# Attention stage of a one-core encoder: the decode tile moved inside each head, the two maps of differential attention scored one after the other, and the first head's loads cut in halves

## The reference, cut to what matters

```python
# A, stick-breaking
w = exp(log_sigmoid(z) + after)          # after: reversed cumulative sum of -softplus(z)
# B, sliding window of 128 with sinks; the two query chunks of a tile see 2 blocks of keys at most
p = softmax(concat[s + bias, sink])[:-1]
# C, differential: two maps of 32 dimensions for each head, one shared V
w = softmax(s[0] + bias) - lam * softmax(s[1] + bias);  out = rmsnorm(w @ v, gain)
# D, forgetting
p = softmax(s + f_q - f_k)
```

## Time and profile before

| | us |
|---|---|
| median of 3 runs (1962.41 to 1962.87) | 1962.59 |
| the profiled execution | 1961.66 |
| its span from first to last instruction | 1959.9 |
| PE busy in the span | 1828.4 |
| DVE busy | 850.5 |
| ACT busy | 650.0 |
| the stretch from 350 to 900 us, which holds the attention stage: PE busy | 475.32 of 550 |

### The profile page before, as it was taken

How to read it: one execution, slowest core, us unless ns; L and a number is a source line. 1 busy time by engine, 2 the same in 40 slices (tenths; PEclk the granted TensorE clock), 3 DMA queues, 4 the chain that set the end, 5 groups by cost and what they waited for, 6 DMA issues and landing times. The chain is left out here.

```text
span 1959.9 us, 27322 instructions
## 1 busy us (share of the span) xinstructions
PE 1828.4 (93%) x10459; PEld 1637.6 (84%) x10459; DVE 850.5 (43%) x1619; ACT 650.0 (33%) x1387; POOL 85.1 (4%) x169
## 2 busy tenths in 40 slices
PE   6999998588889999979989999999999999998998
PEld 6999996477777787868889898989898989996886
DVE  4333331666665666543543333333333333333434
ACT  5322321566554444442332121212121222221335
POOL 0000000000000010011010000000000000000000
PEclk9999999699899999979989999999999999999999
DMA  5666841756456745625231111111111111112102
GB/s 178 210 226 218 269 170 67 154 122 138 97 121 146 146 103 132 148 60 184 70 126 44 43 44 44 43 44 43 43 43 44 43 43 43 43 44 66 50 28 99
DMA packets 152165, 195.20 MB, mean 100 GB/s; under 512 B 42980, under 2 KB 106148, under 8 KB 152024
## 3 DMA queue, kind: packets, MB, share of 16 engines
q1 hardware_dynamic: 105352, 131.63, 25.8%
q10 hardware_dynamic: 39136, 36.05, 5.5%
q0 software_dynamic: 7552, 25.76, 4.0%
HBM read 143.17 MB, written 54.81 MB: 101 GB/s over the span
## 5 line engine op out<-in xcount | busy, mean ns | idle before, releaser
L113 PE MATMUL up<-xt_hi,w_hi_even 128*128 128x384 f32 x768 | 258.0, 336 | 2.0 <-PEq L1444 1.8
L115 PE MATMUL up<-xt_hi,w_lo_even 128*128 128x384 f32 x768 | 257.8, 336 | 0.0
L114 PE MATMUL up<-xt_lo,w_hi_even 128*128 128x384 f32 x768 | 257.6, 335 | 0.0
L115 PE MATMUL down<-w_hi_odd_b,hidden_lo 128*128 128x512 f32 x576 | 224.5, 390 | 0.0
L114 PE MATMUL down<-w_lo_odd_b,hidden_hi 128*128 128x512 f32 x576 | 224.5, 390 | 0.0
L113 PE MATMUL down<-w_hi_odd_b,hidden_hi 128*128 128x512 f32 x576 | 224.0, 389 | 0.0
L1665 DVE TENSOR_TENSOR h_rows<-down,h_rows 128x1024 f32<-128x1024 f32 x72 | 88.2, 1225 | 236.8 <-PE down L115 236.8
L1630 ACT ACTIVATE hidden_rows<-up 128x384 f32<-128x384 f32 x96 | 47.3, 492 | 418.0 <-PE up L115 418.0
L1658 DVE TENSOR_TENSOR hidden_rows<-hidden_rows 128x384 f32<-128x384 f32 x96 | 53.6, 558 | 224.3 <-ACT hidden_rows L1630 224.3
L113 PEld LDWEIGHTS up<-xt_hi,w_hi_even 128*128 128x128 f32 x768 | 145.0, 189 | 3.6 <-DVE xt_lo L140 2.2
L114 PEld LDWEIGHTS up<-xt_lo,w_hi_even 128*128 128x128 f32 x768 | 145.0, 189 | 0.8
(11 more groups left out here) (264 smaller groups left out, 3522.0 us busy)
## 6 DMA issues: line engine op xcount, KB each, us to landing
w_raw<-w_up SPq DMA_DIRECT2D x64, 256.0 KB, 2.9
w_raw<-w_down SPq DMA_DIRECT2D x64, 256.0 KB, 3.2
w_raw<-w_in SPq DMA_DIRECT2D x24, 256.0 KB, 4.5
head_rows<-head_out ACTq DMA_DIRECT2D x16, 288.0 KB, 3.8
head_rows_in<-head_rows POOLq DMA_DIRECT2D x9, 512.0 KB, 4.4
x_rows<-x_prompt SPq DMA_DIRECT2D x8, 512.0 KB, 3.6
w_raw<-w_out SPq DMA_DIRECT2D x16, 256.0 KB, 5.5
residual_rows<-x_prompt POOLq DMA_DIRECT2D x16, 256.0 KB, 3.2
```

Of the source, the lines that this page charges most:

```text
L113: nc.tensor.matmul(out, xh, wh, start=first, stop=False)
L114: nc.tensor.matmul(out, xh, wl, start=False, stop=False)
L115: return nc.tensor.matmul(out, xl, wh, start=False, stop=last)
```

## The change

- Order: the first head keeps its order; in the other 15 the sample's tile comes after the tile of 640 keys and before that of 768 (the sixth of nine). `tile(i)` takes the place of `i % TILES`; all that hung on the sample's tile as the last of its head (C's norm, the stores) now hangs on `ends_head`. POOL squares C's outputs before it spreads the next head's new weights, and norms after that. In A, DVE copies the sample's output between the first and the second large operation of the tile three steps later.
- C's maps: for more than 512 keys PE waits for map 0's buffer, issues map 0's matmuls and adds, signals, and then does the same for map 1. Up to 512 keys, and for the sample, the two maps still alternate.
- Fillers: 3 for every tile of C (was 7 for the four wide ones).
- Semaphores: no initial increments and no `primed_sem`; waits for nothing are left out.
- First head: keys and queries come in two halves, 6 transfers of columns 0 to 511, then 6 of columns 512 to 1151. PE starts after the first 6 (`first_in`) and waits for the others ahead of its fifth tile.

```diff
+            FIRST_ORDER = list(range(TILES))
+            LATER_ORDER = [0, 1, 2, 3, 4, SAMPLE, 5, 6, 7]
+            def order(job):
+                return LATER_ORDER if job else FIRST_ORDER
+            def tile(i):
+                return order(i // TILES)[i % TILES]
...
             def is_sample(i):
-                return i % TILES == SAMPLE
+                return tile(i) == SAMPLE
+            def ends_head(i):
+                return i % TILES == TILES - 1
...
-            def at(name, k):
-                return (TILES if name == "o_full" else 1) + k
+            def after(eng, name, k):
+                if k > 0:
+                    eng.wait_ge(q[name], k)
...
                 def _(sp):
-                    sp.wait_ge(primed_sem, 1)
...
+                                if job == 0:
+                                    for cols, loaded in ((slice(0, 512), first_in), (slice(512, TILES * P), done)):
+                                        for part, to in ((0, at_hi), (1, at_lo)):
+                                            sp.dma_start(kt[to:to + half, x, cols].bitcast(F32), k2[g][part][of_k, cols]).then_inc(loaded, 16)
+                                            sp.dma_start(qt[0][to:to + half, x, cols].bitcast(F32), q2[g][part][of_q, cols]).then_inc(loaded, 16)
+                                        for part, to in ((1, at_hi), (0, at_lo)):
+                                            sp.dma_start(qt[1][to:to + half, x, cols].bitcast(F32), q2[g][part][of_q, cols]).then_inc(loaded, 16)
+                                    continue
...
-                    for name in NAMES:
-                        pool.sem_inc(q[name], TILES if name == "o_full" else 1)
-                    pool.sem_inc(primed_sem, 1)
...
                         for job in range(len(JOBS)):
+                            of_c = job and JOBS[job - 1][0] == "C"
+                            if of_c:
+                                squares(job - 1)
                             spread_new(job)
+                            if of_c:
+                                norm(job - 1)
                             if job + 1 < len(JOBS):
                                 spread_operands(job + 1)
-                            if JOBS[job][0] == "C":
-                                norm(job)
...
                         nc.vector.scalar_tensor_tensor(b, z, 0.0, b, ALU.max, ALU.add).then_inc(q["a_sp"], 1)
+                        if between is not None:
+                            out(between)
...
+                        if i == 0:
+                            pe.wait_ge(first_in, 16 * 6)
+                        if (i == 4 if job == 0 else t == 0):
+                            job_loaded(pe, job)
...
+                        if g == "C" and n > 512:
+                            for m in maps:
+                                bank_free(m)
+                                products([m])
+                                add(m)
+                            return
+                        for m in maps:
+                            bank_free(m)
...
-                        wide = 4 <= t < SAMPLE
...
-                        for _ in range({"A": 3 if t >= 3 else 1, "B": 2, "C": 7 if wide else 3, "D": 0}[g]):
+                        for _ in range({"A": 3 if t >= 3 else 1, "B": 2, "C": 3, "D": 0}[g]):
```

More of the change, by code:

```diff
@@ L784, in keys @@
             def keys(i):
-                n = P * (i % TILES + 1)
+                n = P * (tile(i) + 1)
                 if is_sample(i):
@@ L1171, in maximum @@
                                 src = probs(i)
-                                nc.vector.scalar_tensor_tensor(src[:, 0:n], score(i, m)[:, 0:n], fq[:, odd(i), i % TILES:i % TILES + 1], cs[odd(i)][:, 0:n],
+                                nc.vector.scalar_tensor_tensor(src[:, 0:n], score(i, m)[:, 0:n], fq[:, odd(i), tile(i):tile(i) + 1], cs[odd(i)][:, 0:n],
                                                                ALU.add, ALU.subtract).then_inc(q["f_scores"], 1)
-                                dve.wait_ge(q["f_scores"], at("f_scores", sum(gated(y) for y in range(i + 1))))
+                                after(dve, "f_scores", sum(gated(y) for y in range(i + 1)))
                             if g != "B":
@@ L1312, in scores @@
-                            pe.wait_ge(q[f"ks_in{e}"], at(f"ks_in{e}", 16 * sum(cache_loads(JOBS[x][0]) for x in range(e, job + 1, 2))))
+                            after(pe, "spread", 3 * (job + 1))
+                            after(pe, f"ks_in{e}", 16 * sum(cache_loads(JOBS[x][0]) for x in range(e, job + 1, 2)))
                         maps = range(2 if g == "C" else 1)
                         n_own = {m: (slice(HD * m, HD * m + HD) if g == "C" else slice(0, P)) for m in maps}
-                        befores = [score_before(UNIT[(i, m)]) for m in maps]
@@ new lines, in add, with products @@
+                        def add(m):
+                            for c, unit_, mat in added(i):
+                                last = nc.tensor.matmul(score(i, m)[:, c:c + mat.shape[-1]], unit_, mat, start=False, stop=True, skip_group_check=True)
+                            last.then_inc(q["s_full"], 1)
+                        def products(turns):
+                            k0 = P * first_block(i)
+                            for c in range(0, n, 512):
+                                w = min(512, n - c)
+                                for part in range(2):
+                                    for m in turns:
+                                        own = n_own[m]
+                                        nc.tensor.matmul(score(i, m)[:, c:c + w], qt[part][own, e, P * t:P * (t + 1)],
+                                                         kt[own, e, k0 + c:k0 + c + w], start=part == 0, stop=False, skip_group_check=True)
@@ L1331, in scores @@
                         else:
-                            k0 = P * first_block(i)
-                            for c in range(0, n, 512):
-                                w = min(512, n - c)
-                                for part in range(2):
-                                    for m in maps:
-                                        own = n_own[m]
-                                        nc.tensor.matmul(score(i, m)[:, c:c + w], qt[part][own, e, P * t:P * (t + 1)],
-                                                         kt[own, e, k0 + c:k0 + c + w], start=part == 0, stop=False, skip_group_check=True)
+                            products(maps)
                         for m in maps:
-                            for c, unit_, mat in added(i):
-                                last = nc.tensor.matmul(score(i, m)[:, c:c + mat.shape[-1]], unit_, mat, start=False, stop=True, skip_group_check=True)
-                            last.then_inc(q["s_full"], 1)
+                            add(m)
                     def turn_back(i):
-                        pe.wait_ge(q["ot_read"], at("ot_read", i // TILES + 1))
-                        pe.wait_ge(q["o_read"], at("o_read", i))
+                        after(pe, "ot_read", i // TILES + 1)
+                        after(pe, "o_read", i)
                         nc.tensor.transpose(OP[:, HD * (i % 2):HD * (i % 2 + 1)], ot[:, :], ident[0:HD, 0:HD]).then_inc(q["o_full"], 1)
```

154 lines of the change are left out of this document (79 added, 75 removed).

## The result

The changed kernel takes **1986.08 us** (median of 4 runs, 1983.85 to 1986.68) against 1962.50 (4 runs, 1957.19 to 1962.87): ratio 1.0124, 95% interval 1.0105 to 1.0144. It is slower by 23.6 us; 1941 was forecast, with 1955 as the upper end. The profiled execution took 1983.85, its span is 1981.9. Where a kernel has single executions more than 1.5% above its fastest, its median counts them and its ratio does not.

A forecast was written before the change was run, and what follows sets the result against it. Only the attention stage changes, PE busy 475 of 550 us, with limits differing by head (C's wide tiles: a three-engine chain). Savings 6.2 + 12 + 1.4 + 2 = 21.6 us gave 1941.0; main case 1935 to 1948, wider range 1931 to 1955.

The forecast's parts named there:

- start: First head: PE starts 8.4 us earlier, then stands 3 us for cached values; 6.2 us kept, bounds 4.3 and 8.4.
- split of the maps: C's wide tiles: map 0's earlier scores shorten the chain by 1.4 us a head at most, -0.5 at the lower end.
- order in A and B: A and B heads: gains and losses nearly cancel; 2 us saved over seven later heads, between -3 and +6.
- order in C and D, with the end: D, C pairs: seam waits go; 3.0 us a pair including the split, 12 for four, plus 1.4 after the last D.
- map 0's scores start when map 0's exponential is done: C's wide tiles, one by one: map 0's scores start some 1.1 us before map 1's.
- behind that only map 1's own remain: C's 1024 keys: after map 1's exponential, only its scores, 1.07 us, and 0.25 for map 0's rest; 0.4 us go.
- The first rival: Split worth nothing, seams little: ACT's copy waits for transposes behind both maps, so the chain keeps its length; 1953, chance 0.20.
- The 2.8: C's wide tiles: extra PE time a head from unpaired matmuls, 2 x 3328 columns at 2.4 GHz, in us.
- PE stands for about 1.9 us: Seam D to C: DVE makes the next C's bias before D's tile of 1024 keys, and PE waits about 1.9 us.
- the prediction's own sign: Stage: prediction wrong if clock slices show more sixes and sevens, or the D, C pair stays above 67 us.
- the clock's rival: C's wide stretches: fewer fillers and half the array let PE's clock fall; 2036 whole, 1988 half; chance 0.06.
- The argument from D: Against the clock falling: D has no fillers, yet keeps 1.00 with PE busy 14.23 of 16 us, transposes in each step.

The follow-up runs named there:

- e4: Kernel before with only the changed start (old order, maps in turns, seven fillers): 1956.9 us, ratio 0.9988.
- e7: Changed kernel with the old order and C's maps in turns, three fillers kept: 1952.9 us, ratio 0.9968.
- e1: Changed kernel with the old order in every head, split and three fillers kept: 1959.9 us, ten runs from 1944 to 1995.
- e10: e7 with the new order in A and B: 1958.3 us, ratio 0.9995.
- e12: Changed kernel with C's maps in turns again, new order and three fillers kept: 1971.0 us, ratio 1.0065.
- e8: Changed kernel with the sample's tile last again in the heads of D alone: 1970.4 us.
- e9: Changed kernel with ten fillers at D's last tile but one and four more at each of A's seventh and eighth tiles: 1970.3 us.
- e11: e10 with four more fillers in each of A's last two places: 1954.3 us, ratio 0.9971.
- e2: Changed kernel with the new order in A and B alone, old order in C and D: 1988.7 us, four runs from 1960.4 to 1996.5.
- e3: Changed kernel with the new order in C and D alone, old order in A and B: 1979.8 us.
- e5: Changed kernel with seven fillers in C's wide tiles again, order and split kept: 1988.2 us.

## Why the prediction was wrong

The terms, from the kernels that differ by one part (over before, one part after the other):

| part | forecast | measured | from |
|---|---|---|---|
| start | -6.2 | -2.9 | e4 |
| fewer fillers, maps in turns | (with the split) | -4.5 | e7 - e4 |
| split of the maps, beside the old order | -5.6 with fewer fillers | +7.5 (0 without e1's three longest runs) | e1 - e7 |
| order in A and B | -2 | +5.6 | e10 - e7 |
| order in C and D, with the end | -7.8 | +12.7 | e12 - e10 |
| split, beside the new order | | +12.7 | changed - e12 |

The second, fourth, fifth and sixth rows and the start add up to the +23.6. The last two are clear of the noise; the one for A and B is at its edge, and those for the start and for the fewer fillers are within it.

- **Start**: right in its mechanism and in its time at the fifth scores (6.2 us). At least half of it did not reach the end; in e4's profile the second head of A took 2.6 us of it back at a lower clock, and nothing was left at the attention's end. The halves of 128 KB landed 2.6 to 2.9 us after their issue; the Trainium skill's rule ("DMA: Bandwidth & Descriptors", section Bandwidth, batch to 1 MiB) did not hold them up here.
- **Split**: "map 0's scores start when map 0's exponential is done" held. The step that failed is the next one, "behind that only map 1's own remain": 1.07 us, and 0.25 for map 0's rest. For 1024 keys PE needed 2.2 us from the end of map 1's exponential (751.48 on ACT) to the transposes (753.66) in e1, and with the maps in turns 1.9 (744.49 to 746.42 in e7). Since ACT's copy and next exponentials wait for these transposes, the chain grew by 0.1 us a tile instead of falling by 0.2 to 0.4, and by 1.3 where the sample's tile follows. The first rival (the split worth nothing) had this chain right, and its price too low. Behind it stands PE's work, up by 4.6 us a head where 2.8 was forecast. The 2.8 counted columns only; what it leaves out is about 0.1 us at the first product of each map (0.34 us to the next one, 750.63 to 750.97, where others take 0.22 to 0.24) and 0.1 on the way to the biases (0.33), twice a tile instead of once; that is about half of the 0.45 us a tile that the columns leave unexplained. "TensorEngine Tiling (Array Packing)", Key Properties, of the Trainium skill says that changing the tiling mode drains TensorE. These rows do not show that it is this: D's first product of 512 columns, with 128-row matmuls on both sides, takes 0.31 us as well (703.04 to 703.35 in e7), and only the step to the biases is shorter there (0.23).
- **Order in C and D**: the failed step is the seam. "PE stands for about 1.9 us" was 3.55, since the chain behind the bias (gated scores, maximum, exponential of 1024 keys) was not added to it, and "at full clock" was not so: the fall to 1.2 GHz behind that wait cost 4.1 us more, a little over the wait itself. e8 (wait gone, first pair 69.2) and e9 (exponential as late, clock held by fillers, the two next steps 4.1 us shorter) show both.
- **Order in A and B**: A did get 0.4 us shorter (31.5 us on average, against 31.9 for a head at full clock before), but B behind it runs at 0.81 to 0.87 and 2 to 4 us longer. The exact wait that starts this was not isolated; four fillers more at each of two places near A's end bring B1 to 1.00 (B2 stays at 0.88) and give 4 us back (e11).
- **The rivals**: the prediction's own sign came true, the pair stayed above 67 us (75.3). The time came out where the clock's rival has it (1988, given 0.06), but not by its way: it has the clock fall in C's wide tiles, and these ran at 0.99 to 1.00 in all four heads. The clock fell at the seams after waits, and in the last head of C it stayed low through the four narrow tiles; the split and the wait made up the rest. That the number came out is luck. That the rival's own case exists is shown by e2 (54.4 against 42.4 us), where the wide tiles do run at 0.50. Why in one execution and not in the next stays open. So does the rule of the Trainium skill on transposes ("TensorE: Matmul & The Clock Gate", Part 4: PE-mode transpose), which I weighed against D's row and set aside: no run separates transposes from the rest. The argument from D was too weak, as it was one head without a wait.

## What to carry to other kernels

Before moving a light tile away from a seam, ask what the seam then waits for: here the last unit of one head frees the buffer of the next head's first, so the lightest tile belongs there. A wait of TensorE can cost twice, once itself and once in the clock behind it; so cost the steps behind a wait that a change creates (here 3.5 us) at both levels. Before giving up pairs of half-array matmuls for an earlier start of one of them, follow the chain to what the next engine waits for: an early start is worth nothing if that stands behind both.

## What the runs showed of the hardware

- The same kernel took 1944 and 1995 us on the same chip (e1), with mean granted clocks of 0.978 and 0.949; the runs of others (e3, e5, four each) lie within 4 us.
- PE can be busy for 6.00 of 6 us and stay at 1.2 GHz for 24 us (742 to 766 in e2), with half-array products, transposes, fillers and the matmuls of the values in it. The fall in front came behind waits of 0.42 and 0.21 us only.
- Matmuls of 512 columns that compute nothing, ten where PE waited at the seam to C and eight more near A's end, made a kernel 13 us faster (e9).
